# First norm by feature, with two tiles and the gates' columns worked behind the modulation stages

## The reference, cut to what matters

```python
mod = silu(c) @ w_ada + b_ada
sh1, sc1, g1, sh2, sc2, g2 = split(mod, 6)
h = rmsnorm(x, norm_mix) * (1.0 + sc1) + sh1
y = mixer(h, ...)        # proj = h @ w_in: hq, hf, hi, hog, gq, gk, gv, ga, gb, gz, gate_a, gate_b
x = x + g1 * y
h = rmsnorm(x, norm_ffn) * (1.0 + sc2) + sh2
x = x + g2 * swiglu(h, w_up, w_down)
return rmsnorm(x, final_norm), states
```

## Time and profile before

| | |
|---|---|
| median of three runs | 949.81 us |
| the profiled execution | 951.82 us, its span 950.0 us |
| VectorE busy | 669.4 us (70%) |
| ScalarE busy | 438.2 us (46%) |
| GpSimd busy | 105.6 us (11%) |
| moved by DMA | 104.88 MB, 110 GB/s in the mean |
| mean granted clock of TensorE | 0.997 |

### The profile page before, as it was taken

One profiled execution on the slowest core, in us unless ns is written; L12 is line 12 of the kernel. 1 busy time (PEld: TensorE's weight loads), 2 busy tenths in 40 slices (PEclk: granted clock), 3 DMA queues, 4 the chain that ended last, 5 costly groups with the idle time before them and its releaser, 6 DMA issues.

```text
span 950.0 us, 22427 instructions
## 1 busy us (share of the span) xinstructions
PE 923.8 (97%) x9425; PEld 892.8 (94%) x9425; DVE 669.4 (70%) x1254; ACT 438.2 (46%) x808; POOL 105.6 (11%) x133
## 2 busy tenths in 40 slices
PE   6999999999999999999999999999999999999997
PEld 6999888989999999999999999999999999999996
DVE  3778879866577677477766888889435899994553
ACT  6687445424223544553222257465322666662213
POOL 0110011112020110100100001122001222220000
PEclk9999999999999999999999999999999999999998
DMA  9834234444333432315643332232233343323222
GB/s 347 268 87 134 59 97 112 113 128 117 115 102 102 123 85 68 100 56 165 208 127 106 90 89 77 80 90 73 85 96 104 102 119 91 90 78 101 67 67 95
DMA packets 146175, 104.88 MB, mean 110 GB/s; under 512 B 5170, under 2 KB 139000, under 8 KB 144924
## 3 DMA queue, kind: packets, MB, share of 16 engines
q1 hardware_dynamic: 139099, 79.23, 28.6%
q0 software_dynamic: 6352, 22.00, 7.7%
q10 hardware_dynamic: 624, 2.23, 0.6%
HBM read 100.12 MB, written 3.31 MB: 109 GB/s over the span
## 4 chain that ended last, share of the span: by engine, by line
PE 48%; DVE 4%; ACT 3%; issue 2%; POOL 0%; DVEq 0%; ACTq 0%; POOLq 0%
PE G L2153 31%; PE G L2243 16%; DVE x_lo L1680 1%; DVE w_sum L1691 1%; DVE sum_lo L1700 1%; PE R L2164 0%; ACT w_hi L1306 0%; DVE w_lo L1700 0%; ACT w_hi L1219 0%; ACT b L1286 0%; ACT d_hi L1311 0%; POOL w_sum L1164 0%; PE R L2161 0%; DVE val L1711 0%; DVE w_lo L1592 0%
## 5 line engine op out<-in xcount | busy, mean ns | idle before, releaser
L2153 PE MATMUL G<-h_hi,w_hi 128*128 128x272 f32 (+1 forms) x880 | 263.7, 300 | 2.8 <-DVE ff_shift L2099 1.4
L2153 PE MATMUL G<-h_lo,w_hi 128*128 128x272 f32 (+1 forms) x880 | 253.8, 288 | 0.4 <-issue 0.4
L2153 PE MATMUL G<-h_hi,w_lo 128*128 128x272 f32 (+1 forms) x880 | 253.5, 288 | 0.1
L1592 DVE TENSOR_TENSOR w_lo<-raw,w_hi 128x1024 fp32r<-128x1024 f32 (+2 forms) x111 | 117.2, 1056 | 104.4 <-ACT w_hi L1219 103.6
L2153 PEld LDWEIGHTS G<-h_hi,w_hi 128*128 128x128 f32 x880 | 165.7, 188 | 6.2 <-DVE ff_shift L2099 1.7
L2153 PEld LDWEIGHTS G<-h_lo,w_hi 128*128 128x128 f32 x880 | 166.0, 189 | 0.6 <-issue 0.6
L2153 PEld LDWEIGHTS G<-h_hi,w_lo 128*128 128x128 f32 x880 | 165.7, 188 | 0.0
L1219 ACT ACTIVATE w_hi<-raw 128x1024 fp32r<-128x1024 f32 (+2 forms) x111 | 101.4, 914 | 90.6 <-PE G L2153 90.5
L1164 POOL TENSOR_TENSOR w_sum<-raw 128x512 f32<-128x512 f32 x36 | 50.1, 1395 | 318.3 <-DMA raw<-in_w_up 169.8
L2243 PE MATMUL G<-x_hi,sum_hi 128*128 128x272 f32 x288 | 83.7, 291 | 1.2 <-ACT partial L1322 1.1
L2243 PE MATMUL G<-x_hi,sum_lo 128*128 128x272 f32 x288 | 83.4, 290 | 0.0
(11 more groups left out here) (326 smaller groups left out, 2074.2 us busy)
## 6 DMA issues: line engine op xcount, KB each, us to landing
raw<-in_w_in SPq DMA_DIRECT2D x48, 512.0 KB, 4.1
raw<-in_w_up SPq DMA_DIRECT2D x44, 512.0 KB, 4.0
w_ada<-in_w_ada_t POOLq DMA_DIRECT2D x49, 256.0 KB, 3.2
wada<-in_w_ada_s SPq DMA_DIRECT2D x8, 1024.0 KB, 14.3
raw<-in_w_down SPq DMA_DIRECT2D x16, 320.0 KB, 3.2
raw<-in_w_out SPq DMA_DIRECT2D x8, 512.0 KB, 4.1
raw<-in_w_down SPq DMA_DIRECT2D x8, 512.0 KB, 4.1
w_ada_t<-in_w_ada_t POOLq DMA_DIRECT2D x15, 256.0 KB, 3.2
```

The source lines that it names most:

```text
L1592: dve.tensor_tensor(lo, raw[:, i % RAW, 0:job.nk, 0:job.m], hi.bitcast(F32), ALU.subtract).then_inc(w_lo_done, 1)
L2153: ins = pe.matmul(out, w, x, start=(job.first and k == 0 and p == 0), stop=(job.last and k == job.nk - 1 and p == 2))
```

## The change

x comes from the host in feature order (`x_t`, which the kernel has used for its later reload of x) straight into xT, two values of k at a time. `in_sq` squares each k on ScalarE and adds up on VectorE; `in_sums` sums over the partitions with a matrix of ones and takes the reciprocal root (544 columns, Ln and Exp on ScalarE); `in_norm(k)` multiplies xT's k-th slice with it on VectorE. x_sq, x_first, xtok and x_diag are gone.

The first pair is now gk0 and gk1, and the gates' columns are a third job that is multiplied into two banks of R (`gab_part`: six values of k behind the third stage, the last two behind the pair). In the stages the order of the steps is another one: `in_norm` of two slices, `split(j)` (the weights of job j), two groups of products, `ada_rows(j)`, a third group, `ada_T(j)`, the fourth group. The weights of gq0, job 3, are split into a place of their own. Fills between the stages use two banks instead of four (`bank_of`, `user_before`). The gates' columns come from the host as an array of their own. The stages' loads have the three first jobs' weights between them. Behind the pair ScalarE evacuates gk0, the gates and gk1 before the next job; the steps of the gates and of the first norms come one job later, and the solve of the first pair is woven with one tile less.

The diff, cut to its core:

```diff
-    for c in range(3):
-        do("x_sq", c)
-    do("x_first", 0)
...
     do("vectors")
-    do("x_first", 2)
+    for k in range(KD):
+        do("in_sq", k)
+    do("in_sums")
     do("c_cols")
-    do("x_first", 3)
-    do("x_first", 4)
+    do("in_norm", 0)
+    do("in_norm", 1)
     do("split", 0)
-    do("split", 1)
     do("ada_rows", 0)
     do("ada_T", 0)
     do("h1", 0)
     for j in range(1, STAGES):
+        do("in_norm", 2 * j)
+        do("in_norm", 2 * j + 1)
+        do("split", j)
+        do("duo_part", 2 * j - 2, 0)
+        do("duo_part", 2 * j - 2, 1)
         do("ada_rows", j)
-        do("duo_part", 2 * j - 2, 0)
+        do("duo_part", 2 * j - 1, 0)
         do("ada_T", j)
-        do("duo_part", 2 * j - 2, 1)
-        do("duo_part", 2 * j - 1, 0)
         do("duo_part", 2 * j - 1, 1)
         if j == STAGES - 1:
-            do("split_hi", 2)
+            do("gab_part", 0)
         do("h1", j)
-    do("split_lo", 2)
     do("sel")
...
     gk0, gk1, gq0, gq1, gv0, gv1 = gdn_inputs(0)
-    duo(gagb, gk0)
-    around(gk1, [("g_sp",), ("split_hi", 4), ("g_a",), ("split_lo", 4)], [])
-    around(gq0, [("g_sq", 0, 2), ("g_scan",)], [])
-    around(gq1, [("g_sq", 0, 3), ("g_norm", 0, 2)], [("g_rows",), ("c_load",)])
-    around(gv0, [("g_sq", 0, 0), ("g_norm", 0, 3)], [("g_bcast", 0)])
-    around(gv1, [("g_sq", 0, 1), ("g_norm", 0, 0), ("g_rel", 0)], [])
+    mark = len(plan)
+    for one in (gk0, gk1, gagb):
+        one()
+    evac = [s for s in plan[mark:] if s[0] == "evac"]
+    del plan[mark:]
+    plan.append(("duo", 0, 1))
+    do("gab_part", 1)
+    plan.extend([evac[0], evac[2], evac[1]])
+    around(gq0, [("g_sp",), ("split_hi", 4), ("g_a",), ("split_lo", 4)], [])
+    around(gq1, [("g_sq", 0, 2), ("g_scan",)], [])
+    around(gv0, [("g_sq", 0, 3), ("g_norm", 0, 2)], [("g_rows",), ("c_load",)])
+    around(gv1, [("g_sq", 0, 0), ("g_norm", 0, 3)], [("g_bcast", 0)])
     gk0, gk1, gq0, gq1, gv0, gv1 = gdn_inputs(1)
-    around(gk0, [("g_norm", 0, 1)], [])
+    around(gk0, [("g_sq", 0, 1), ("g_norm", 0, 0), ("g_rel", 0)], [])
+    around(gk1, [("g_norm", 0, 1)], [])
...
-    weave(gdn_steps(0, ahead), parts_of(gk1, gq0, gq1, gv0, gv1, *hg_inputs("hf", 0), fine=True))
+    weave(gdn_steps(0, ahead), parts_of(gq0, gq1, gv0, gv1, *hg_inputs("hf", 0), fine=True))
...
-            while plan[at][0] not in ("job", "g_y", "g_u"):
+            while plan[at][0] not in ("half" if g == 1 else "job", "g_y", "g_u"):
                 at += 1
             plan[at + 1:at + 1] = [("taps", g, 0), ("taps", g, 1)]
...
+        def bank_of(f):
+            f0, gf = first_fill[spot("ada_rows", 0)], first_fill[spot("gab_part", 1)]
+            return 2 + f % 2 if f0 <= f < gf else f % 4
...
-            load(0)
-            load(1)
+            sp.dma_start(ones[:, :], t["all_ones"]).then_inc(ones_in, 16)
             for j in range(STAGES):
                 for v in range(2):
                     sp.dma_start(wada01[:, j, v, :, :], t["w_ada_s"][j, v]).then_inc(ada_in[j], 16)
+                if j <= gab:
+                    load(j)
...
+            for j in range(STAGES):
+                act.dma_start(xT[:, 2 * j:2 * j + 2, :], t["x_t"][:, 2 * j:2 * j + 2, :]).then_inc(x_in[j], 16)
...
@@ ScalarE @@
+                elif name == "in_sq":
+                    act.wait_ge(x_in[k // 2], 16)
+                    if k >= 2:
+                        act.wait_ge(in_added, max(k - 2, 1))
+                    act.activation(sq[:, k % 2, :], xT[:, k, :], ACT.Square).then_inc(in_squared, 1)
...
@@ VectorE @@
+                elif name == "in_sq":
+                        dve.tensor_tensor(acc[:, :], sq[:, 0, :] if k == 1 else acc[:, :], sq[:, k % 2, :], ALU.add)\
+                            .then_inc(in_added, 1)
+                elif name == "in_norm":
+                    dve.wait_ge(in_rn_ready, 1)
+                    dve.tensor_tensor(xT[:, k, :], xT[:, k, :], in_rn[:, :], ALU.mult).then_inc(in_normed, 1)
...
@@ TensorE @@
+                elif name == "gab_part":
+                    for k in (range(KD - 2), range(KD - 2, KD))[a[0]]:
+                        for p, (w, x) in enumerate(((hi, h_hi), (hi, h_lo), (lo, h_hi))):
+                            for half in range(2):
+                                ins = pe.matmul(R[0:QUAD + NH, bank_of(f + half), 0:HALF], w[:, k, :],
+                                                x[:, k, half * HALF:(half + 1) * HALF], start=(k == 0 and p == 0),
+                                                stop=(k == KD - 1 and p == 2))
```

More of the change, by code:

```diff
@@ L542, in bank_users @@
     return {
-        "vectors": ["dve"] * 2, "x_first": ["act", "dve"] if name == "x_first" and a[0] < N_CHUNK else ["act"], "sums": ["act"] * 2, "onorm": ["act"] * 2,
+        "vectors": ["dve"] * 2, "in_sums": ["act"] * 2, "gab_part": ["act"] * 2 if a[:1] == (1,) else [], "sums": ["act"] * 2, "onorm": ["act"] * 2,
         "ada_rows": ["act"], "ada_T": ["dve"], "g_rows": ["dve"], "g_norm": ["act"] * 2, "g_bcast": ["act"] * n, "g_gram": ["dve"] * n,
@@ L573, in build @@
     for kind, _, _ in groups:
+        if kind == "gagb":
+            slot_freed.append(None)
+            continue
         count[GROUP_USER[kind]] += 1
@@ L580, in build @@
     duos = [s[1:] for s in plan if s[0] == "duo"]
-    gab = duos[0][0]
-    aside = {gab: "rec", duos[1][1]: "ffn"}
+    gab_group = next(g for g, x in enumerate(groups) if x[0] == "gagb")
+    gab = groups[gab_group][2]
+    aside = {gab: "rec", gab + 1: "third", duos[1][1]: "ffn"}
     ending = len(groups) - 1
@@ L694, in build @@
                             at("rec", "gab_lo", [P, KD, m0], F32R, off=base + 38 * row + 512 + KD * m0 * 4)))
+        w_aside["third"] = (at("rec", "third_hi", [P, KD, P], F32R, off=base + 46 * row),
+                            at("rec", "third_lo", [P, KD, P], F32R, off=base + 46 * row + KD * P * 4))
         o_gate_z = at("rec", "o_gate_z", [P, 2, TOK])
@@ L800, in build @@
         ident_in = sem("ident_in")
-        x_in = [sem(f"x_in{c}") for c in range(CHUNKS)]
+        x_in = [sem(f"x_in{j}") for j in range(STAGES)]
+        ones_in = sem("ones_in")
         x_again = sem("x_again")
@@ L1000, in slot_of @@
         def slot_of(g):
-            return (g + sum(groups_before[f] <= g and (run_last[f] - f + 1) % 2 for f in groups_before)) % 2
+            return (g + (g > gab_group) + sum(groups_before[f] <= g and (run_last[f] - f + 1) % 2 for f in groups_before)) % 2
         def run_before(g):
@@ L1141, in _ @@
                     pool.memset(T64[0:P // 2, :, :], 0.0).then_inc(inverse_zero, 1)
-                    wait_group(pool, groups_at["gagb", 0])
+                    pool.wait_ge(fill_done, last_bank[spot("gab_part", 1)] + 1)
                     pool.memset(Um[:, :, :, :], 0.0).then_inc(inverse_zero, 1)
@@ L1214, in split_weights @@
                     return
-                if i in aside:
+                if aside.get(i) == "ffn":
                     act.wait_ge(job_done, i - 2)
-                elif nth_ring[i] >= 2:
+                elif i not in aside and nth_ring[i] >= 2:
                     act.wait_ge(job_done, ring[nth_ring[i] - 2] + 1)
@@ L1387, in _ @@
                     ln_exp_tables()
-                    wait_slot(act, groups_at["gagb", 0])
+                    wait_bank(act, last_bank[spot("gab_part", 1)])
                     act.activation(rows[:, 2, :], acc[QUAD:QUAD + NH, :], ACT.Exp, scale=-1.0)
@@ L2046, in _ @@
                     if kind == "gagb":
-                        wait_slot(dve, g)
+                        wait_bank(dve, last_bank[spot("gab_part", 1)])
                         dve.wait_ge(sp_log, 1)
@@ L2266, in _ @@
                     fill(n, 1, [tr(lambda b: R[:, b, 0:NB], vecs[0:NB, 1, :])])
[L2267 to L2273 removed]
+                elif name == "in_sums":
+                    pe.wait_ge(ones_in, 16)
+                    pe.wait_ge(in_added, KD - 1)
+                    sums_of(n, 0, acc)
+                elif name == "gab_part":
+                    f = first_fill[spot("gab_part", 1)]
+                    if a[0] == 0:
+                        wait_bank(pe, user_before(f))
+                        wait_bank(pe, user_before(f + 1))
+                        pe.wait_ge(w_lo_done, nth_split[gab] + 1)
+                    hi, lo = weights(gab)
+                    for k in (range(KD - 2), range(KD - 2, KD))[a[0]]:
+                        if k + 1 > seen["lo"]:
+                            pe.wait_ge(lo_ready, k + 1)
+                            seen["lo"] = k + 1
+                        for p, (w, x) in enumerate(((hi, h_hi), (hi, h_lo), (lo, h_hi))):
+                            for half in range(2):
+                                ins = pe.matmul(R[0:QUAD + NH, bank_of(f + half), 0:HALF], w[:, k, :],
+                                                x[:, k, half * HALF:(half + 1) * HALF], start=(k == 0 and p == 0),
+                                                stop=(k == KD - 1 and p == 2))
```

(6 more changed lines are left out.)

124 lines of the change are left out of this document (50 added, 74 removed).

## The result

The changed kernel takes 989.6 us (median; 988.2 to 992.1), beside 950.35 of the kernel before (949.5 to 953.2) on the same chip: 1.0411 times as long, with an interval from 1.0392 to 1.0430. Slower was forecast, but 969 and not 990, and the range ended at 977. Half of the loss was not in the sum.

A forecast was written before the change was run, and what follows sets the result against it. TensorE, busy for 97% of the span, was taken to bound the kernel. Stages 9.4, gap behind them 7.7, lag 0.7 and clock 1.3 sum to 19.1, on 949.81 giving 969; range 957 to 977.

The forecast's parts named there:

- The stages: Modulation stages: closed loop from h_lo through TensorE to h1, 7.0 a stage, stage 1 longer; gq0 at 57.9, +9.4.
- The first norm: Start of the kernel: sums and first rows at the lower clock, h1(0) at 22.4 against 22.73, gaining 0.3.
- Behind the stages: After gq0: TensorE waits for w_lo of gq1 behind a ScalarE and VectorE chain of 13.7, +7.7.
- Lag and clock behind the gap: Tiles after the wait for gq1's weights: engines' lag +0.7 and a dropped clock +1.3.
- The solve beside six tiles: First pair's solve with six tiles instead of seven: cost between nothing and 6; nothing taken, 3 for the range.
- Rival 3: Lower clock holds through stages 2 and 3 as well; with 3 from the solve, 973 to 982; chance 0.12.
- Rivals 1 and 2: 1 (0.12): clock stays up, 963.4; 2 (0.10): gap behind the stages much smaller than 7.7, 955 to 962.
- rival 5: Whole kernel: the waits and the first norm's gain cancel, time within 0.2%; chance 0.04.
- Rival 4: Stages: loads, not waits, set the pace, `ada_rows(j)` starts at its landing; 1.5 faster, 948.3; chance 0.06.

The follow-up runs named there:

- e1: Changed kernel with `ada_rows(j)` ahead of its stage's products again: 981.7 us, ratio 1.0311 to the kernel before.
- e6: Changed kernel with four useless matmuls ahead of the first norm's sums and two behind them: 986.4 us, ratio 1.0361.
- e7: Changed kernel with `vectors` behind the squares in the plan instead of ahead of them: 988.6 us, ratio 1.0405.
- e9: Changed kernel with 24 useless products ahead of each half of gq0: 989.1 us, ratio 1.0385.
- e2: Changed kernel with the weights of gq1 split right behind the first evacuation (gk0): 988.9 us, ratio 1.0397.
- e14: Kernel before with six tiles beside the first solve, and eight small VectorE modulation pieces moved behind Tc's copy and the state's update: 957.96 us, ratio 1.0077.
- e4: Kernel before with only gk1 of the second pair moved ahead of the first solve, leaving six tiles beside it: 968.9 us, ratio 1.0185.
- after: The changed kernel itself, with the whole change and no follow-up edit: 989.6 us, ratio 1.0411 to the kernel before.
- e11: Kernel before with the norm by feature alone, vectors behind the squares, two useless matmuls ahead of the sums and two behind: 950.7 us, ratio 0.9992.

## Why the prediction was wrong, point by point

**The stages: right.** From h1(0) to gq0 the working has 35.5 (22.4 to 57.9); it took 36.2. Single numbers: 7.0 a stage against 7.23, 12.3 for stage 1 against 12.7. e1 takes the closed loop away (h1(1) then comes 6.2 behind h1(0)), and 0.0100 of the ratio (9.5 us) with it.

**The first norm: mechanism right, size off by 3.1.** h1(0) at 25.5, not 22.4. The sums (2.31) and rows (3.64) at the lower clock are as worked out or 0.7 more; e6 prices the whole of it at 2.6. What I missed is 2.4: `vectors` stands ahead of the additions in VectorE's program and waits for the head scalars' load and two transposes (7.76 to 8.6). The last addition was put at x's landing plus 2.5, as if VectorE had nothing ahead of it. e7 shows it, 15.0 to 12.6.

**Behind the stages: right.** Wait of 7.1 for 7.7, chain of 13.4 (61.7 to 75.1) for 13.7, at the place that was named. e9 shows that TensorE's work has no part in it. What the working left unsaid, e2 shows: with the weights of gq1 split ahead of the gates' chain the wait only moves to the next tile, and no gain is clear of the noise. The 7.7 was a debt of both engines and not of one place in the order. Lag and clock behind the gap came to 0.8, not 2.0.

**The solve beside six tiles: the step that failed.** The working gave it a cost between nothing and 6, took nothing, and put 3 into the range. It cost 19.2 here and 18 alone. Two things make up the 18, by e14 against e4 and before: 7, about the text's own bound of one tile's 6.0, since the solve has no slack (57.7 from N to S with seven tiles, 59.5 with six); and 10 to 11 that no bound of the text held, since it looked only at how much work runs beside the chain and not at where the shared engine's other work falls. VectorE runs its program in order. With one tile less, the taps of every following tile meet other steps of the solve, and the modulation's pieces that had been put into the holes by hand stood ahead of Tc and S. Behind the first of these waits the clock fell, for 15 us in after. Of the 19.2 in after 6.0 are the tile, and moving the pieces gives back 8.3 in the median; 12.2 came back in its fastest execution. The 4.9 left over are tied to no cause by a run. Rival 3 had a lower clock and 3 for the solve, in the wrong stages and six times too little.

Rivals 1 and 2 fell with the rows at 3.64 and the wait of 7.1, rival 5 with the time. Rival 4 fell: no `ada_rows` starts at its landing; those of stages 1 to 3 have no idle time ahead of them. In e11 the last stage's rows do start at its landing (33.16 and 33.1), which is why an earlier h1(0) is worth so little in the old plan.

The sum as it should have been: 9.4 + 3.1 + 0.7 at the front, 7.4 + 0.8 behind it, 19.2 in the solve: 40.6.

## What to carry to other kernels

When a tile is taken out of a hand-set weave, don't price only its own length as cover: list what stands in each engine's program ahead of the few instructions that the chain waits for, with every later tile shifted, and expect a bunch. Moving eight small pieces was worth 10 to 11 us in one plan and cost 4 to 5 in the other, so such a placement is part of the plan's order and has to be made anew with it. And useless work is a cheap probe: 48 products that cost nothing tell that TensorE is not what sets the pace there, before one looks for what does.

## What the runs showed of the hardware

Two falls of the clock behind idle times of the same length lasted very differently. In the changed kernel TensorE stood idle twice in a stretch with many 32x32 matmuls:

```profile
142.70 0.60 PE L2176 MATMUL G<-h_lo,w_hi 128*128 128x272 f32 x1 [2.50 <-issue]
...
155.76 0.94 PE L2184 MATMUL R<-Tc,N 32*32 32x32 f32 x32 [2.56 <-DVE Tc L1655]
```

Behind the first the products took 0.43 each, and 0.29 again from 146 us on. Behind the second the granted clock was 0.50 from 157.5 to 172.5 while the records show TensorE busy for all 15.0. Why the two differ no run shows. The Trainium skill ("TensorE: Matmul & The Clock Gate", section "HAM oscillation — how this bites in real kernels") describes a wait that drops the clock, so that the work behind it starts at the lower one. Both falls agree with it in kind; each fall ends there within the block of work behind the wait, and the second one here outlasts 15.0 us of it.

At the start the column of the granted clock reads high while the matmuls show the lower one: in after the digit of the first slice is 9, and there the first 64 matmuls of `ada_rows` take 3.64. There the durations of a known instruction are the better witness (1.95 and 3.64, 1.16 and 2.31), not the column.

With the useless matmuls (6.54 and 1.96 us of records) the sums and the first rows ran at the full clock, across an idle time of 1.33 between them; the first products at 25 us were slow again (0.43 each in place of 0.29) after an idle time of 2.60.
